# Gates' product ahead of the value projection in a two-block sequence kernel on one Trainium2 core

## The chip, the core and the metric

The program runs on one core of one Trainium2 chip. TensorE multiplies, VectorE (DVE), ScalarE (ACT) and GpSimd (POOL) do the rest, and the SyncE queue (SP) starts most of the transfers. Each engine runs its own list of instructions in order and waits for semaphores that others raise. The metric is the device time in microseconds (us) of one execution; lower is better.

## What is computed

Two transformer-like blocks over 512 tokens of width 1024, in float32. The change lies in the first block, in one wide projection and what hangs on it:

```python
h = rms_norm(x, norm_mix_g) * (1.0 + sc1) + sh1
proj = einsum("bsd,de->bse", h, w_in) + b_in
glu_in, qk_in, v, o_pre, if_pre, merge_pre = split(proj, IN_SPLITS)

a = glu_in[..., :1024] * sigmoid(glu_in[..., 1024:])
a = causal_depthwise_conv(a, conv_dw_w, conv_dw_b)       # 31 taps, 1024 channels
a = silu(layer_norm(a, conv_ln_g, conv_ln_b))            # then w_conv_pw

qk = silu(causal_depthwise_conv(qk_in, qk_conv_w, qk_conv_b))   # 4 taps
hm = mlstm_chunkwise(q, k / 16, v, i_pre, f_pre)         # 4 heads of 256
```

`mlstm_chunkwise` needs, from the 8 gate columns `if_pre`, `log_sigmoid(f_pre)` (computed as min(f, 0) - ln(1 + exp(-|f|))), its running sum b, and a running maximum m of i - b: the decays. They weigh the scores of each head.

## The kernel before

Each product with a weight is made exact enough by cutting weight and activation in a high and a low part and adding three products (high by high, low by high, high by low). Channels lie on partitions, 512 tokens side by side, so one tile of 128 output channels is 24 matmuls of 128x512 from one weight unit of 128x1024; the value projection `w_v` has tokens on partitions instead and takes four units in each of its two blocks, which fill four PSUM banks at a time.

A weight unit is loaded by SP into one of four `raw` buffers; ACT copies it to `sph` (the high part, L2103), one of three buffers. The low part `spl` is made in one of two ways: by a subtraction on DVE (L2464), or, for the units in `BY_DMA`, by a negated copy on ACT (L2106) and an adding DMA that POOL issues (L3102). The unit of the gates, `w_if`, has eight columns; its low part lies in the other half of the same `sph` buffer (L2459) and its product is 16 matmuls (L1932).

The function `plan()` writes the order by hand: it walks through the tiles, and after each third of a tile `between()` lets background work step forward: `later_ops` (operations put off by a tick), `side` (generators, one step for each tick), and `spare`, a queue of single taps of the 31-tap convolution (L2523, L2526, on DVE). `rate[1]` is the number of taps for each tick. Every engine then gets its part of this one list, in that order.

Around the change the order is this: eight pairs of convolution tiles; the value blocks 0 and 1 (units 16 to 23) with 3.2 taps a tick; the gates' product (unit 24); then head 0's tiles z = 0 to 3 (units 25 to 28), head 1's tiles from unit 29 on, and so forth. After the gates' product ACT copies one half (L2136), DVE adds the other (L2549), and ACT runs `gates` (L2142 to L2151: two biased copies, Abs, Exp, Ln, the last two each with a table load). The generator `decays()` puts `log_forget` (L2555), four steps `decay` (L2564 to L2572, one for each 128 tokens), the copies `decay_rows` (L2579, L2582, L2587) and the transposes `decay_cols` beside the tiles that follow. A head's tile goes through ACT (L2159, L2162), three taps on DVE (L2597) and ACT again (L2167). The value tiles leave their banks on DVE (L2543, `vtok`).

PSUM banks come from two rings, `main` and `misc`. Two banks are lent from `misc` to `main` during the convolution tiles and the value blocks, and go back afterwards. A tile that takes a bank waits until its last user has emptied it. `fence(name)` marks a place that other engines' first writes to reused memory wait for.

Of the kernel before, what the change touches and what calls it, by code (L numbers as in the profile page):

```python
# [24 lines left out]
for _name, _n in [("b_ada", 48), ("g_mix", 8), ("b_glu", 16), ("b_qk", 16), ("b_o", 8), ("b_mg", 16),  # L25
# [16 lines left out]

GMIX, GFFN = 0, 72

BY_DMA = (*range(6, 24),)

WHOLE = (0, 1, 2, 3,)

ATTEND = (3, 2, 0, 7)

ORDER = [(0, 0), (0, 1), (0, 2), (1, 0), (0, 3), (1, 1), (1, 2), (1, 3)]
TAPS = [[0, 0, 0, 1], [1, 1, 1, 1], [1, 1, 1, 1], [1, 1, 1, 1], [1.6, 1.6, 1.6, 1.6], [1.6, 1.6, 1.6, 1.6],
        [1.6, 1.6, 1.6, 1.6], [1.6, 1.6, 1.6, 1.6]]

LENT = 2
# [32 lines left out]
class Signals:  # L88
# [11 lines left out]
    def up(self, name, *labels, by=1):  # L100
        self.count[name] = self.count.get(name, 0) + by
        for label in labels:
            assert label not in self.now, label
            self.now[label] = (name, self.count[name])
        return self.sem(name), by

    def at(self, *label):
        if not self.known:
            return None
        name, value = self.known[label]  # L110
        return self.sem(name), value
# [18 lines left out]
def plan():  # L130
# [3 lines left out]
    def add(name, *args):  # L134
        steps.append((name, args))

    main, misc, tmp = Ring(0, 4), Ring(4, 4), Ring(0, NT)
# [8 lines left out]
    def keepc(n):  # L146
        kept[0] += n
        assert kept[0] <= 176
        return kept[0] - n

    def fence(name):
        add("fence", name)
# [6 lines left out]
    def load():  # L159
        add("load", W["loaded"])  # L160
        W["loaded"] += 1
# [3 lines left out]
    def split():  # L165
# [9 lines left out]
        if n in WHOLE:  # L175
            W["owed"] += 1
            return
        add("split", n, "dma" if n in BY_DMA else lo_engine[0])
        load()
# [32 lines left out]
    def ready(eng=None, more=0):  # L212
        was = lo_engine[0]
        lo_engine[0] = eng or was
        while W["cut"] < W["finished"] + W["ahead"] + more:
            split()
        lo_engine[0] = was

    def take(name, tile, first, size):
        units.append((name, tile, first, size))  # L220
        W["used"] += 1
        ready()
        return W["used"] - 1

    def done():
        W["finished"] += 1


    side, tail, spare, later_ops = [], [], [], []
    rate, due, tick = [0, 0], [0.0], [0]  # L230
# [18 lines left out]
    def between():  # L249
        while later_ops and later_ops[0][0] <= tick[0]:  # L250
            later_ops.pop(0)[1]()
        tick[0] += 1
        step(rate[0])
        due[0] += rate[1]
        background(int(due[0]))
        due[0] -= int(due[0])
# [3 lines left out]
    def new_tile():  # L260
        tiles[0] += 1
        return tiles[0] - 1
# [98 lines left out]
    def gemm_halves(src, acts, evac):  # L361

        b, free = main.take()
        g = new_tile()
        n = take(src, 0, 0, 1024)
        for half in range(2):
            for k0 in (0, 4):
                add("side_by_side", b, acts, n, half, k0, free, [("unit", n), ("tile", g)] * (half and k0 == 4))
                if not half:
                    if k0 == 0:  # L370
                        ready(more=1)
                    between()
        done()
        main.give(b, *evac(b, g))
        between()

    def gemm_tok(src, block, kt, acts, evac):
        banks = [main.take() for _ in range(T)]
        g = new_tile()
        for k0 in range(0, kt, 2):  # L380
            n = take(src, block, k0 * 512, 1024)
            for k in range(2):
                last = k0 + k == kt - 1
                add("tok", banks, acts, n, k, k0 + k, last, [("unit", n)] * (k == 1) + [("tile", g)] * last)
                if k == 0:
                    ready(more=1)
                    between()
            done()
            if k0 + 2 < kt:
                between()  # L390
        for t in range(T):
            main.give(banks[t][0], *evac(t, banks[t][0], g))
        between()
# [52 lines left out]
    def spread(name, src, after):  # L446
        b, bfree = misc.take()
        add("spread", name, src, b, bfree, after)
        return b
# [15 lines left out]
    def rows_of(ss, width, between=(), behind=()):  # L465
        b = spread(ss.name, ("small", root_of(ss, width, *between)), [("rs", ss.name)])
        if behind:
            warm(*behind)
        return b
# [68 lines left out]
    for i in range(8):  # L538
# [4 lines left out]
        j, free = tmp.take()  # L543
# [75 lines left out]
    fence("v")  # L619
    add("v_begin")  # L620

    for blk in range(2):
        def evac(t, b, g):
            add("v", blk, t, b, g)
            return [("v", blk, t)]
        gemm_tok("w_v", blk, 8, "n1", evac)

    def gates(b, g):
        j, free = tmp.take()
        k, free2 = tmp.take()  # L630
        add("gates_low", b, g, k, free2)
        add("gates_sum", b, j, free, k)
        later_ops.append((tick[0] + 1, lambda: add("gates", j, k)))
        forget.extend((j, k))
        return [("gate", "sum")]

    forget = []
    gemm_halves("w_if", "n1", gates)
    misc.free += [main.take() for _ in range(LENT)]
    cb, gd, mus = keepc(40), keepc(16), keepc(8)  # L640

    def decays():
        yield
        yield
        add("log_forget", *forget)
        for j in forget:
            tmp.give(j, ("lf",))
        k1, free = tmp.take()
        fence("decay")
        add("decay_begin", k1, free, mus)  # L650
        for t in range(T):
            add("decay", t, k1, mus)
            yield
        tmp.give(k1, ("decay", 3))
        add("m_out")
        for k in range(T):
            add("decay_rows", k)
            yield
        for _ in range(5):
            yield  # L660
        b, free = misc.take()
        add("decay_cols", b, free, cb, gd)
        misc.give(b, ("cb",), ("gd",))

    side.append(decays())


    fence("qk")
# [72 lines left out]
    def heads(h):  # L741
# [3 lines left out]
        for z in range(4):  # L745
            i = 2 * h + z % 2 + (8 if z >= 2 else 0)
            rate[:] = [1, TAPS[h][z]]
            used = qk_used[(h + 1) % 2] + ([("decay_tr",)] if h == 1 else [])
# [50 lines left out]
    def gates_on(h):  # L799
        for z in range(4):  # L800
            rate[:] = [1, TAPS[4 + h][z]]
            i = 2 * h + z % 2
# [262 lines left out]
    b = spread("x1", ("small", root), [("rs", "x1")])  # L1065
# [277 lines left out]
    for i in range(4):  # L1343
        b, free = misc.take()
# [50 lines left out]
    b = spread("mix", ("small", r), [("rs", "mix")])  # L1395
# [72 lines left out]
    b = rows_of(ssf, D, (320,), (512, 512))  # L1468
# [24 lines left out]
def program(nc, A, out, known):  # L1493
    steps, units = plan()
    ctx = ExitStack()
    with ctx:
# [8 lines left out]
        def place(name, off, shape, dt=F32):  # L1505
            return nc.alloc_sbuf_tensor_at(name, shape, dt, offset=base + off)
# [29 lines left out]
        TMP = [place(f"tmp{i}", o + 2048 * i, [128, S]) for i in range(NT)]; o += 2048 * NT  # L1536
# [65 lines left out]
        def vec(name, i, p=slice(0, 128)):  # L1602
            return V_[p, VEC[name] + i:VEC[name] + i + 1]
# [113 lines left out]
        def fenced(name, *engines):  # L1717
            return [at("fence", name, e) for e in engines or ("PE", "ACT", "DVE", "POOL")]
# [15 lines left out]
        def run(program_of):  # L1734
            for name, args in steps:
                if name in program_of:
                    program_of[name](*args)
# [357 lines left out]
        def _(e):  # L2095
            w = Waited(e, G)
            up, fence = follow("ACT")
# [40 lines left out]
            def gates(j, k):  # L2138
                p = slice(32, 36)
                z, y = TMP[j], TMP[k]  # L2140
                w.wait_ge(at("gate", "sum"), *fenced("v"))
                e.activation(IR[:], z[0:4, :], ACT.Identity, bias=vec("b_if", 0, slice(0, 4))).then_inc(  # L2142
                    *up("s_if", ("gate", 0)))
                e.activation(z[p, :], z[p, :], ACT.Identity, bias=vec("b_if", 0, p)).then_inc(
                    *up("s_if", ("gate", 1)))
                w.wait_ge(at("gate", 1))
                e.activation(y[p, :], z[p, :], ACT.Abs).then_inc(*up("s_if", ("gate", 2)))
                w.wait_ge(at("gate", 2))
                e.activation(y[p, :], y[p, :], ACT.Exp, scale=-1.0).then_inc(*up("s_if", ("gate", 3)))
                w.wait_ge(at("gate", 3))  # L2150
                e.activation(y[p, :], y[p, :], ACT.Ln, bias=1.0).then_inc(*up("s_if", ("gate", 4)))  # L2151
# [279 lines left out]
            def pg(i, b, g, j, free):  # L2431
# [1 line left out]
                e.activation(TMP[j][:], P_[b][:], ACT.Sigmoid, bias=vec("b_pg", i)).then_inc(  # L2433
                    *up("s_gate", ("pg_gate", i)))

            run({"begin": begin, "split": split, "csil": csil, "square": square, "rsqrt": rsqrt, "root_table": root_table, "glu": glu, "gates": gates, "gates_low": gates_low, "rope_rows": rope_rows, "decay_cols": decay_cols, "qk": qk,
                 "qk_silu": qk_silu, "score": score, "vals": vals, "head_scale": head_scale, "turn": turn,
                 "gate_mul": gate_mul, "gc": gc, "gc_gate": gc_gate, "ln_mean": ln_mean, "ln_out": ln_out, "pw": pw, "norm": norm, "gmix": gmix, "round": round_,
                 "silu_table": silu_table, "seven_full": seven_full, "seven_t_high": seven_t_high, "seven_high": seven_high, "seven_first": seven_first, "seven_third_copy": seven_third_copy,
# [866 lines left out]
```

## Time and profile before

| | us |
|---|---|
| median of 3 runs | 1557.66 |
| lowest, highest | 1556.52, 1559.5 |
| the profiled execution | 1556.89 |
| its span in the trace | 1555.1 |

Mean granted clock of TensorE: 0.992 of full. Busy shares of the span: TensorE's matmuls 98%, weight loads 83%, DVE 73%, ACT 52%, POOL 10%, DMA queues together about 46% of the 16 engines. The time of the profiled execution is the span and 1.8 us around it. In a timeline each row is a run of equal instructions: its start, its length, engine, line, what it writes and reads and how many; brackets name the idle time before it and who ended that. A matmul's end is modelled, so a row of matmuls is longer than the distance to the next one's start.

### The profile page before, as it was taken

The numbers are of one execution on the slowest core, as the hardware profiler recorded it, in microseconds if no ns is written. First come the engines' busy times: TensorE is split into PE (matmuls) and PEld (weight loads), VectorE is DVE, ScalarE is ACT, GpSimd is POOL, SyncE is SP. The second block draws the span as 40 slices with busy tenths as digits, with TensorE's granted clock in tenths as the row PEclk, the third lists the DMA queues.
The fourth block names the chain that finished last, engine by engine and source line by source line (L and its number), as shares of the span: only waits on it lengthen the run. The fifth ranks groups of instructions, "written<-read, shape, count | busy, mean of one in ns | idle before, by whom it ended". The sixth has DMA issues, their size and how long they took to land.

```text
span 1555.1 us, 21650 instructions
## 1 busy us (share of the span) xinstructions
PE 1522.9 (98%) x8256; PEld 1297.4 (83%) x8256; DVE 1140.3 (73%) x1852; ACT 805.1 (52%) x1292; POOL 151.3 (10%) x158
## 2 busy tenths in 40 slices
PE   8999899999999999999899999999999999999998
PEld 3788777877888899999688887778887999998877
DVE  8998898898788789888464447766578888854356
ACT  5543578765543656666333335446456666643223
POOL 0111000000000101111011001000202111100000
PEclk9999999999999999999999999999999999999999
DMA  9788221222566547755533323110325555573331
GB/s 371 178 188 208 69 95 61 75 95 90 209 237 209 162 123 198 196 150 156 160 111 91 119 74 118 63 48 28 115 82 184 150 150 158 156 236 116 98 135 68
DMA packets 66490, 215.17 MB, mean 138 GB/s; under 512 B 7757, under 2 KB 10061, under 8 KB 65618
## 3 DMA queue, kind: packets, MB, share of 16 engines
q1 hardware_dynamic: 52496, 179.68, 33.8%
q0 software_dynamic: 13888, 34.09, 11.4%
q8 instruction: 66, 1.08, 0.3%
q14 instruction: 38, 0.31, 0.1%
q10 hardware_dynamic: 2, 0.00, 0.0%
HBM read 175.99 MB, written 8.40 MB: 119 GB/s over the span
## 4 chain that ended last, share of the span: by engine, by line
PE 47%; DVE 3%; ACT 1%; issue 1%; DMA 1%; SPq 0%; DVEq 0%; ACTq 0%
PE bank L1875 10%; PE bank L1876 10%; PE bank L1883 9%; PE bank L1913 4%; PE bank L1915 4%; PE bank L1923 4%; PE bank L2045 1%; PE bank L2058 1%; DMA tmp<-in_pos 1%; PE bank L2051 1%; PE bank L2072 1%; PE bank L2065 1%; PE bank L1953 0%; PE bank L1954 0%; PE bank L1955 0%
## 5 line engine op out<-in xcount | busy, mean ns | idle before, releaser
L1875 PE MATMUL bank<-HH,sph 128*128 128x512 f32 x840 | 339.5, 404 | 9.4 <-DVE spl L2464 7.7
L1876 PE MATMUL bank<-HH,spl 128*128 128x512 f32 x840 | 330.0, 393 | 0.0
L2464 DVE TENSOR_TENSOR spl<-raw,sph 128x1024 fp32r<-128x1024 f32 (+2 forms) x162 | 201.5, 1246 | 161.6 <-ACT sph L2103 161.4
L2103 ACT ACTIVATE sph<-raw 128x1024 fp32r<-128x1024 f32 (+1 forms) x183 | 187.1, 1025 | 163.0 <-PE bank L1883 124.0
L1883 PE MATMUL bank<-HL,sph 128*128 128x512 f32 x840 | 222.8, 397 | 0.0
L1875 PEld LDWEIGHTS bank<-HH,sph 128*128 128x128 f32 x840 | 159.4, 190 | 47.2 <-issue 11.9
L1876 PEld LDWEIGHTS bank<-HH,spl 128*128 128x128 f32 x840 | 159.4, 190 | 34.5 <-issue 1.4
L1883 PEld LDWEIGHTS bank<-HL,sph 128*128 128x128 f32 x840 | 156.6, 188 | 34.8 <-issue 2.4
L2526 DVE SCALAR_TENSOR_TENSOR convout<-convin,vecs,convout 128x512 f32<-128x512 f32 x240 | 165.0, 745 | 0.0
L1913 PE MATMUL bank<-HH,sph 128*128 128x256 f32 x592 | 148.7, 283 | 0.1
L1915 PE MATMUL bank<-HH,spl 128*128 128x256 f32 x592 | 148.4, 283 | 0.0
L1875 PE MATMUL bank<-midh,sph 128*128 128x512 f32 x352 | 138.0, 392 | 7.2 <-DVE spl L2464 7.2
L1876 PE MATMUL bank<-midh,spl 128*128 128x512 f32 x352 | 137.7, 391 | 0.0
L1913 PEld LDWEIGHTS bank<-HH,sph 128*128 128x128 f32 x592 | 113.6, 192 | 0.7 <-ACT tmp L2282 0.5
L1915 PEld LDWEIGHTS bank<-HH,spl 128*128 128x128 f32 x592 | 113.6, 192 | 0.1
L1913 PE MATMUL bank<-th,sph 128*128 128x256 f32 x444 | 111.5, 283 | 0.2 <-ACT tmp L2277 0.2
L1915 PE MATMUL bank<-th,spl 128*128 128x256 f32 x444 | 111.3, 283 | 0.0
L2776 DVE TENSOR_TENSOR spl<-raw,sph 128x512 fp32r<-128x512 f32 x148 | 100.0, 696 | 10.7 <-ACT sph L2272 10.6
L2272 ACT ACTIVATE sph<-sums 128x512 fp32r<-128x512 f32 x111 | 65.1, 621 | 71.5 <-DVE sums L2763 71.5
L1923 PE MATMUL bank<-HL,sph 128*128 128x256 f32 x592 | 95.2, 283 | 0.0
L2272 ACT ACTIVATE sph<-raw 128x512 fp32r<-128x512 f32 x148 | 92.2, 623 | 4.2 <-PE bank L1923 1.2
L1883 PE MATMUL bank<-midl,sph 128*128 128x512 f32 x352 | 87.6, 389 | 0.0
(365 smaller groups left out, 2715.5 us busy)
## 6 DMA issues: line engine op xcount, KB each, us to landing
raw<-in_w_in SPq DMA_DIRECT2D x69, 512.0 KB, 3.3
raw<-in_w_up SPq DMA_DIRECT2D x66, 512.0 KB, 4.5
more<-in_w_ada SPq DMA_DIRECT2D x32, 512.0 KB, 5.4
raw<-in_w_down SPq DMA_DIRECT2D x32, 512.0 KB, 3.7
raw<-in_w_gate SPq DMA_DIRECT2D x22, 512.0 KB, 3.6
raw<-raw POOLq DMA_DIRECT2D x37, 256.0 KB, 4.4
midl<-tmp POOLq DMA_DIRECT2D x37, 256.0 KB, 3.3
spl<-raw POOLq DMA_DIRECT2D x18, 512.0 KB, 5.9
```

Of the source, the lines that this page charges most:

```text
L1875: e.matmul(P_[b][:], sph(n)[:, q], hi[:, k, :], start=k == 0, stop=False)
L1876: e.matmul(P_[b][:], spl(n)[:, q], hi[:, k, :], start=False, stop=False)
L1883: m = e.matmul(P_[b][:], sph(n)[:, q], low[:, k, :], start=False, stop=last and k == kb - 1)
L1913: e.matmul(to, high_of(which, s)[:, q], x, start=begins and k == 0, stop=False, skip_group_check=not begins)
L1915: e.matmul(to, low_of(which, s)[:, q], x, start=False, stop=False, skip_group_check=not begins)
L1923: m = e.matmul(to, high_of(which, s)[:, q], x, start=False, stop=k == 3, skip_group_check=not begins)
L2045: e.matmul(P_[b][:, 0:wide], QH[:, h, token(t)], KH[:, h, 0:wide], start=True, stop=True).then_inc(*up("s_score", ("mla_mm", h, t)))
L2103: e.activation(sph(n), raw(n), ACT.Copy).then_inc(*up("s_w_high", ("wh", n)))
L2272: e.activation(high_of(which, s), given, ACT.Copy).then_inc(*up("s_w_high", ("seven_high", which, s), *labels))
L2464: e.tensor_tensor(spl(n), raw(n), sph(n).bitcast(F32), ALU.subtract).then_inc(*up("s_w_low", ("wl", n)))
L2526: ins = e.scalar_tensor_tensor(CO[:, i, :], src, wt, CO[:, i, :], ALU.mult, ALU.add)
L2776: e.tensor_tensor(low_of(which, s), given, high_of(which, s).bitcast(F32), ALU.subtract).then_inc(*up("s_w_low", ("seven_low", which, s), ...
```

## The change

The gates' product goes from behind the value blocks to ahead of them, so `w_if` is now unit 16 and the value units are 17 to 24; `BY_DMA` moves with that, and the number of units cut by DMA stays 18. Of the gates' activations the Exp and Ln stand two ticks later than the first three, in a step of their own (`gates_log`). `decays()` starts beside value block 0. The taps beside the value blocks go from 3.2 a tick to 1.5 (gates' product), 1.4 (block 0) and 3.2 (block 1), and the tiles of head 0 get 1.3, 1.3, 1.3 and 2.3 a tick where they had 0, 0, 0 and 1. The two lent banks go back after value block 1.

```diff
-BY_DMA = (*range(6, 24),)
+BY_DMA = (*range(6, 16), *range(17, 25),)
...
-TAPS = [[0, 0, 0, 1], [1, 1, 1, 1], [1, 1, 1, 1], [1, 1, 1, 1], [1.6, 1.6, 1.6, 1.6], [1.6, 1.6, 1.6, 1.6],
+VALUE_TAPS = (1.4, 3.2)
+TAPS = [[1.3, 1.3, 1.3, 2.3], [1, 1, 1, 1], [1, 1, 1, 1], [1, 1, 1, 1], [1.6, 1.6, 1.6, 1.6], [1.6, 1.6, 1.6, 1.6],
...
-    for blk in range(2):
-        def evac(t, b, g):
-            add("v", blk, t, b, g)
-            return [("v", blk, t)]
-        gemm_tok("w_v", blk, 8, "n1", evac)
...
         later_ops.append((tick[0] + 1, lambda: add("gates", j, k)))
+        later_ops.append((tick[0] + 3, lambda: add("gates_log", k)))
...
+    rate[:] = [1, 1.5]
     gemm_halves("w_if", "n1", gates)
-    misc.free += [main.take() for _ in range(LENT)]
...
     def decays():
-        yield
-        yield
+        k1, free = tmp.take()
+        fence("decay")
+        add("decay_begin", k1, free, mus)
+        for _ in range(4):
+            yield
         add("log_forget", *forget)
         for j in forget:
             tmp.give(j, ("lf",))
-        k1, free = tmp.take()
-        fence("decay")
-        add("decay_begin", k1, free, mus)
...
     side.append(decays())
+
+    for blk in range(2):
+        def evac(t, b, g):
+            add("v", blk, t, b, g)
+            return [("v", blk, t)]
+        rate[:] = [1, VALUE_TAPS[blk]]
+        gemm_tok("w_v", blk, 8, "n1", evac)
+
+    misc.free += [main.take() for _ in range(LENT)]
...
+            def gates_log(k):
+                p, y = slice(32, 36), TMP[k]
                 w.wait_ge(at("gate", 2))
                 e.activation(y[p, :], y[p, :], ACT.Exp, scale=-1.0).then_inc(*up("s_if", ("gate", 3)))
```

What this makes of the order is seen best on DVE, beside value block 1. Names there: `vtok<-bank` empties a value block, `convout<-convin` is a tap, `spl<-raw,sph` the low part of a weight unit, `sph_60<-raw_54` that of the gates' unit. Before, from block 0's emptying to block 1's:

```order
L2543 TENSOR_TENSOR vtok<-bank,vbias 128x2x256 x4
L2526 SCALAR_TENSOR_TENSOR convout<-convin,vecs,convout 128x512 x16
L2459 TENSOR_TENSOR sph_60<-raw_54,sph_60 128x8x64
L2537 TENSOR_TENSOR tmp_90<-tmp_90,convout 128x512 x2
L2523 TENSOR_SCALAR convout<-convin,vecs 128x512 x2
L2526 SCALAR_TENSOR_TENSOR convout<-convin,vecs,convout 128x512 x3
L2464 TENSOR_TENSOR spl_61<-raw_55,sph_58 128x1024
L2526 SCALAR_TENSOR_TENSOR convout<-convin,vecs,convout 128x512 x3
L2543 TENSOR_TENSOR vtok<-bank,vbias 128x2x256 x4
```

Now the same stretch begins with block 0's emptying, the fourth decay step (four instructions) and a tap, and its last 12 groups, from the second of four copies `decay_rows` (`rowc<-`) on, are:

```order
L2587 COPY rowc<-row_138 4x128
L2590 TENSOR_SCALAR rowc<-rowc,row_137 4x128 x2
L2534 SCALAR_TENSOR_TENSOR convout<-convin,vecs,convout 128x512 x4
L2587 COPY rowc<-row_138 4x128
L2590 TENSOR_SCALAR rowc<-rowc,row_137 4x128
L2534 SCALAR_TENSOR_TENSOR convout<-convin,vecs,convout 128x512 x3
L2587 COPY rowc<-row_138 4x128
L2595 TENSOR_TENSOR row_135<-mrow,row_137 4x512
L2534 SCALAR_TENSOR_TENSOR convout<-convin,vecs,convout 128x512 x3
L2472 TENSOR_TENSOR spl_61<-raw_55,sph_58 128x1024
L2534 SCALAR_TENSOR_TENSOR convout<-convin,vecs,convout 128x512 x6
L2472 TENSOR_TENSOR spl_62<-raw_56,sph_59 128x1024
```

Behind these stand four taps and then the emptying of block 1. In all 24 taps, one decay step, all of `decay_rows` and two low parts stand between the two emptyings, where 22 taps, two first taps (L2523), two sums, one low part of a unit and that of the gates stood before.

On DVE at the first head tiles, before, behind the low part of unit 27 (`spl_63`):

```order
L2597 SCALAR_TENSOR_TENSOR tmp_91<-xpad,vecs,tmp_91 128x512 x3
L2555 SCALAR_TENSOR_TENSOR row_136<-tmp_86,tmp_88 4x512
L2564 SCALAR_TENSOR_TENSOR row_137<-tmp_89,row_136 4x128
L2567 TENSOR_TENSOR row_138<-row_135,row_137 4x128
L2569 SCALAR_TENSOR_TENSOR mrow<-row_138,kept 4x128
L2572 TENSOR_TENSOR kept<-mrow,row_137 4x1
L2464 TENSOR_TENSOR spl_61<-raw_54,sph_58 128x1024
```

Now, from the emptying of value block 1 to the same low part of unit 28:

```order
L2551 TENSOR_TENSOR vtok<-bank,vbias 128x2x256 x4
L2545 TENSOR_TENSOR tmp_90<-tmp_90,convout 128x512 x2
L2531 TENSOR_SCALAR convout<-convin,vecs 128x512 x2
L2472 TENSOR_TENSOR spl_63<-raw_57,sph_60 128x1024
L2534 SCALAR_TENSOR_TENSOR convout<-convin,vecs,convout 128x512
L2599 COPY kept<-bank 128x40
L2534 SCALAR_TENSOR_TENSOR convout<-convin,vecs,convout 128x512
L2605 SCALAR_TENSOR_TENSOR tmp_89<-xpad,vecs,tmp_89 128x512 x3
L2534 SCALAR_TENSOR_TENSOR convout<-convin,vecs,convout 128x512 x2
L2472 TENSOR_TENSOR spl_61<-raw_54,sph_58 128x1024
```

The decay steps are gone from this place, and taps stand in it. On PE the first tile of head 0 (unit 25) waited for the second of block 1's four `vtok` instructions before; the rings now hand it a bank that the first of the four empties.

## Rows read from the trace of the kernel before

**Rows 1.** The page: busy time, share of the span, instructions.

```profile
PE 1522.9 (98%) x8256; PEld 1297.4 (83%) x8256; DVE 1140.3 (73%) x1852; ACT 805.1 (52%) x1292; POOL 151.3 (10%) x158
```

**Rows 2.** TensorE's waits, whole span: total, times, longest.

```profile
PE bank L1875 <- DVE spl L2464: 14.9, 3, 7.2
```

**Rows 3.** TensorE's timeline at head 0's tiles: start, length.

```profile
158.04 0.39 PE L1875 MATMUL bank<-HH,sph 128*128 128x512 f32 x1
...
172.54 1.98 PE L1883 MATMUL bank<-HL,sph 128*128 128x512 f32 x8
179.27 0.77 PE L1875 MATMUL bank<-HH,sph 128*128 128x512 f32 x1 [4.75 <-DVE spl L2464]
...
187.38 0.39 PE L1875 MATMUL bank<-HH,sph 128*128 128x512 f32 x1
```

**Rows 4.** Windows after two stalls: busy of PE, PEld, DVE, ACT, POOL; clock; DMA.

```profile
179.27:187.38 8.11, 8.11 (x24) 6.51 (x25) 7.60 (x19) 2.97 (x4) 0.55 (x1) 0.66 0.21 66
1190.46:1196.46 6.00, 6.00 (x19) 4.79 (x20) 5.72 (x8) 2.48 (x5) 2.41 (x2) 0.72 0.33 102
```

**Rows 5.** TensorE's timeline at a shorter stall, later in the program.

```profile
1190.46 0.47 PE L1875 MATMUL bank<-HH,sph 128*128 128x512 f32 x1 [2.99 <-DVE spl L2464]
```

**Rows 6.** DVE's timeline at the head tiles and decays.

```profile
173.10 2.33 DVE L2597 SCALAR_TENSOR_TENSOR tmp<-xpad,vecs,tmp 128x512 f32<-128x512 f32 x3 [4.54 <-ACT tmp L2162]
...
184.05 0.41 DVE L2564 TENSOR_TENSOR_SCAN row<-tmp,row 4x128 f32<-4x128 f32 x1
...
185.39 1.21 DVE L2464 TENSOR_TENSOR spl<-raw,sph 128x1024 fp32r<-128x1024 f32 x1
186.53 0.21 DVE L2579 COPY rowc<-row 4x128 f32<-4x128 f32 x1
...
188.35 2.31 DVE L2597 SCALAR_TENSOR_TENSOR tmp<-xpad,vecs,tmp 128x512 f32<-128x512 f32 x3
190.57 0.21 DVE L2579 COPY rowc<-row 4x128 f32<-4x128 f32 x1
...
191.02 1.21 DVE L2464 TENSOR_TENSOR spl<-raw,sph 128x1024 fp32r<-128x1024 f32 x1
192.16 0.21 DVE L2579 COPY rowc<-row 4x128 f32<-4x128 f32 x1
...
192.90 1.40 DVE L2526 SCALAR_TENSOR_TENSOR convout<-convin,vecs,convout 128x512 f32<-128x512 f32 x2
```

**Rows 7.** DVE's timeline beside value block 1.

```profile
132.85 2.48 DVE L2543 TENSOR_TENSOR vtok<-bank,vbias 128x512 f32<-128x512 f32 x4 [4.63 <-PE bank L1955]
135.25 10.68 DVE L2526 SCALAR_TENSOR_TENSOR convout<-convin,vecs,convout 128x512 f32<-128x512 f32 x16
145.85 0.69 DVE L2459 TENSOR_TENSOR sph<-raw,sph 128x512 fp32r<-128x512 f32 x1
...
154.61 2.48 DVE L2543 TENSOR_TENSOR vtok<-bank,vbias 128x512 f32<-128x512 f32 x4 [0.66 <-PE bank L1955]
```

**Rows 8.** ACT's timeline: the gates' Exp and Ln.

```profile
167.64 1.28 ACT L2149 ACT_TABLE_LOAD   x1
...
170.88 0.63 ACT L2151 ACTIVATE tmp<-tmp 4x512 f32<-4x512 f32 x1
```

**Rows 9.** TensorE's timeline in value block 0: the wait for unit 18.

```profile
121.63 0.50 PE L1953 MATMUL bank<-sph,HH 128*128 128x512 f32 x1 [0.61 <-DMA spl<-raw]
```

**Rows 10.** POOL's timeline: the issue of unit 18's adding DMA.

```profile
113.67 0.86 POOL L3102 DMA_DIRECT2D spl<-raw  x1 [0.32 <-issue]
```

**Rows 11.** Line L3102 from 90 to 150, its ten adding DMAs: time to landing.

```profile
DMA to landing us min/median/max: 4.6/6.1/7.9
```

**Rows 12.** TensorE's waits from 200 to 450: the two longest.

```profile
PE bank L2039 <- DVE tmp L2537: 0.8, 1, 0.8
PE bank L2028 <- DVE sc L2612: 0.8, 1, 0.8
```

**Rows 13.** Window around a TensorE wait of 1.42, columns as in rows 4.

```profile
1030.00:1036.00 6.00, 4.58 (x25) 3.38 (x24) 4.93 (x13) 3.05 (x8) 1.10 (x1) 1.00 0.15 48
```

More of the change, by code:

```diff
@@ L2434, in pg @@
                     *up("s_gate", ("pg_gate", i)))
-            run({"begin": begin, "split": split, "csil": csil, "square": square, "rsqrt": rsqrt, "root_table": root_table, "glu": glu, "gates": gates, "gates_low": gates_low, "rope_rows": rope_rows, "decay_cols": decay_cols, "qk": qk,
+            run({"begin": begin, "split": split, "csil": csil, "square": square, "rsqrt": rsqrt, "root_table": root_table, "glu": glu, "gates": gates, "gates_log": gates_log, "gates_low": gates_low, "rope_rows": rope_rows, "decay_cols": decay_cols, "qk": qk,
                  "qk_silu": qk_silu, "score": score, "vals": vals, "head_scale": head_scale, "turn": turn,
```

## The prediction

> **What bounds the kernel now.** The page comes first: TensorE is busy for 98% of the span [rows 1], so a change can give back only what TensorE idles, and what it loses at a lower clock behind an idle stretch. Next come TensorE's waits by cause: the longest group is three waits for low parts of weights cut on DVE, 14.9 us in all [rows 2]. The three lie at different places; the timeline of the head tiles holds the one this change aims at. There the last matmuls of unit 27 begin at 172.54, and unit 28 begins only at 179.27, after 4.75 idle [rows 3]. The pace: from 158.04 to 172.54 are 64 matmuls in 14.5 us, 0.2266 each, so a unit of 24 is 5.44 and the eight from 172.54 end at 174.35. The stall is 4.92 from issue to issue. The unit behind it takes 187.38 - 179.27 = 8.11 instead of 5.44, at a granted clock of 0.66 on average [rows 4]: 2.67 more, the first part of it at 1.2 GHz. Together 7.59 us.
>
> Why it is there: DVE sat idle 4.54 us until 173.10 for ACT's first qk copy [rows 6], which stood behind the gates' activations with two table loads, 167.64 to 171.51 [rows 8]; behind it DVE ran the logarithm's sum, a decay step, and then unit 28's low part.
>
> **What is removed.** The gates and most decay steps leave the head tiles, so that chain is broken. What comes late instead is counted below. Unit 28's low part now has before it on DVE (from the order) the emptying of block 1 (2.40, 132.85 to 135.25 [rows 7]), some sums and taps, one low part and three qk taps. I follow that further down; it comes out ahead of TensorE. Gain: 7.59.
>
> **What is added: the emptying of value block 1.** This is the main term. Call T0 the time at which TensorE ends block 0. DVE begins to empty it some 0.2 later (132.85 against 132.65, which is 158.04 less 16 and 96 matmuls at 0.2266) and is done 2.40 later. Up to the emptying of block 1 the order gives DVE:
> - 24 taps at 0.6625 (16 from 135.25 to 145.85 [rows 7]): 15.90
> - one decay step, 184.05 to 185.39 [rows 6]: 1.34
> - the copies `decay_rows`: 186.53 to 188.35 is 1.82, 190.57 to 191.02 is 0.45, 192.16 to 192.90 is 0.74 [rows 6]: 3.01
> - two low parts at 1.14 (185.39 to 186.53 [rows 6]): 2.28
>
> The sum is 22.53. Block 1's emptying so begins at T0 + 25.13, its first bank is free after a quarter of 2.48, at T0 + 25.75, and TensorE starts 0.15 after its releaser, as at 179.27. TensorE ends block 1 after 96 matmuls, at T0 + 21.76, and unit 25 needs just that bank (the order: the first of the four, where it was the second before). So TensorE stands still for 25.90 - 21.76 = 4.14 us from issue to issue. Before, DVE was ready 0.66 early at this place [rows 7]. Idle time that DVE has in block 0 does not help, because the chain begins with T0. Both ends of this term lie close: with every dependent step 0.03 shorter it is 3.6; I take 4.14.
>
> **The clock behind it.** A stall of 2.99 [rows 5] was followed by six microseconds at 0.72 [rows 4], a loss of 6 x 0.28 = 1.7; the one of 4.75 cost 2.67. Idle 4.0 (4.14 less the tail of the last matmul) lies between: I take 2.2, bounds 1.7 and 2.7.
>
> **Unit 18.** In block 0 TensorE now waits 0.61 for unit 18's adding DMA [rows 9], issued by POOL at 113.67 [rows 10] and landed 7.9 later, the slowest of the ten [rows 11]. It shares the DMA engines with the next weight load and the bias of the values. POOL's issue hangs on ACT's copies behind the last convolution gate and on a fence there, and neither moves. But the gates' 16 matmuls take 3.63 where unit 16 took 5.44, so TensorE is at unit 18 1.81 earlier. If it lands as late as before, the wait is 0.61 + 1.81 = 2.42; if in the median 6.1, 0.62; in 4.6, none. One adding DMA before it is gone and the load behind unit 17 can start earlier, so I take a landing 1.1 earlier than before, a wait of 1.3. Term: +0.7, bounds -0.6 and +1.8. A wait of 1.42 cost no clock (1.00 [rows 13]); at 2.4 it may, another 1.7 by rows 4, which goes in the upper bound.
>
> A sentence apart: the Trainium skill, DMA: Bandwidth & Descriptors, section Anatomy of one DMA, gives a transfer that GpSimd issues 2.0 us and its bytes over 436 GB/s. As an estimate by that page 512 KB take 3.2 us, unit 18 lands at 116.9, and this term would be -0.6 instead of +0.7. Its section Issuing engines are not separate DMA queues says that transfers of all queues interleave on the same 16 engines; the 7.9 of rows 11 against 4.6 speaks for the second, and no landing in rows 11 is as short as the first.
>
> **The gates' activations and the decays in block 0** cost nothing on the path. ACT runs the first three after DVE's sum of the gates at about 115.5, then one unit's copies, then Exp and Ln in 3.87 (167.64 to 171.51 [rows 8]) from about 121.4 to 125.3. DVE has eight taps (5.3) meanwhile and idles some 4.5. Then `log_forget` and three decay steps with four taps (0.6 + 3 x 1.34 + 4 x 0.66 = 7.3) end at about 132.7, ahead of T0 = 113.9 + 21.8 + 1.3 = 137.0. That cover is 4 us; without it each microsecond moves block 1 one to one. POOL's first write of the decays waits for its fence ahead of unit 20's DMA, by about 118.8; ACT has that unit's copies done at 121.4. The store of m stands ahead of unit 24's DMA and waits for the fourth decay step, T0 + 4, while unit 24's copies end after T0 + 7.5. Unit 16's low part is now cut on DVE at about 101, nine microseconds before it is used.
>
> **The taps in head 0.** With 1.3 taps a tick a tile holds four: DVE needs 4 x 0.66 + 1.14 + 2.22 (the three qk taps, 188.35 to 190.57 [rows 6]) = 6.0 for each 5.44 of TensorE, and for z = 3 seven taps, 8.0. Over four tiles it falls back 26.0 - 21.8 = 4.2. I count from unit 25's start U: low part of unit 28 at U + 14.0, needed at U + 18.5 (with 2.2 for the clock); unit 30: 25.4 against 29.4; unit 31: 33.3 against 34.9; unit 32: 39.3 against 40.3. The margin sinks to about 1 us and no more is asked of it, since from head 1 on the numbers of taps are as before. Cost 0, and a rival.
>
> **Later.** Two taps a tick fewer beside the values are made up one tile later, and the layer norm starts two ticks, 3.6 us, later in TensorE's order. Its mean was waited for 0.8 [rows 12]; DVE's work up to there is the same, so that wait goes: -0.8, bounds 0 and -0.8. The 0.8 beside the scores [rows 12] may go or stay: 0, bounds -0.8 and 0.
>
> **Sum.** -7.59 + 4.14 + 2.2 + 0.7 - 0.8 = -1.35 us. The profiled execution took 1556.89, so it would take 1555.5; the median of the runs lies 0.8 above it, and against that the forecast is 1556.3. All low bounds: -7.6 + 3.6 + 1.7 - 0.6 - 0.8 - 0.8 = -4.5; all high: -7.6 + 4.14 + 2.7 + 1.8 + 1.7 = +2.8. Own range 1553.2 to 1560.4.
>
> **Rivals.**
> - *The stall goes and none comes.* If DVE's row of small decay steps runs much faster between independent taps than alone, and it reaches block 1's bank by T0 + 21.8, the sum is -7.59 + 0.7 - 0.8 = -7.7: 1550.0. Against it: 15.9 of taps and 2.3 of low parts alone leave 1.0 for steps that took 4.35.
> - *Unit 18 lands in time*, with the 4.6 of rows 11: its term is -0.6 for +0.7, the sum -2.65, 1555.0. For it: less traffic before. Against it: the slowest landing was this one. The figure of the Trainium skill's page on DMA, named above, would have it come out so.
> - *Slower: head 0's taps make a second stall.* The margin at units 31 and 32 is 1 us. If DVE comes there more than that late (a longer stall does not help it, a qk copy on ACT that comes late hurts it), TensorE waits again. Price: some 3.0 idle as in rows 5 and 1.7 of clock, 4.7: -1.35 + 4.7 = +3.4, 1561.0. It decides from 1 us of delay on DVE. For it: DVE is over its share in all four tiles. Against it: the count above, by rows, stays positive at each unit.
>
> **How the numbers follow.** Forecast 0.58; no stall 0.13; unit 18 in time 0.15; second stall 0.14. A measurement of this kernel can tell about 0.2%, 3.1 us, from no change. Faster by more than that: all of the first rival, 0.13, four tenths of the second, 0.06, and 0.09 of the forecast's low end: 0.28. Slower: six tenths of the third, 0.08, and 0.02: 0.10. Between: 0.62. The range reaches down to the first rival and up to the middle of the third: 1550.0 to 1560.8.
>
> **What would show it.** In the profile after: TensorE's timeline with one wait of about 4 in front of the first tile of head 0, released by DVE's `vtok`, and a clock near 0.7 behind it; no wait of 4.75 for unit 28; a wait of 0 to 2.4 in block 0 at the second value unit; DVE idle some 4 us in block 0 for the Ln. Wrong would make it: `vtok` of block 1 beginning less than 21.6 us after block 0's end, or any wait for a low part at units 28 to 33.

## The result, and the profile after

Eight runs of each kernel: before 1557.34 us in the median (1556.21 to 1560.54), after 1563.70 (1560.42 to 1566.09). The ratio is 1.0036, with a 95% interval of 1.0024 to 1.0047: slower, by 6.4 us in the medians. The forecast was 1556.3 with a range up to 1560.8; the measured time lies above it. The profiled execution of after took 1561.86 (span 1560.0), 4.97 more than that of before, and the steps are accounted against that difference.

First the page of after, against [rows 1]. The busy times are as good as equal (TensorE 1524.3 for 1522.9), so no work was added; TensorE stands still for longer.

```profile
PE 1524.3 (98%) x8256; PEld 1297.3 (83%) x8256; DVE 1140.7 (73%) x1852; ACT 803.9 (52%) x1291; POOL 150.5 (10%) x158
```

TensorE's waits over the span (total, times, longest), against [rows 2]. DVE's low parts went from 14.9 to 11.9: the 4.75 at unit 28 is gone, and three small waits (1.03, 0.26, 0.21) came. Of the two causes beside them the first is new, and the second had 0.6 before:

```profile
PE bank L1880 <- DVE spl L2472: 11.9, 5, 7.4
PE bank L1880 <- DVE vtok L2551: 4.0, 1, 4.0
...
PE bank L1958 <- DMA spl<-raw: 2.4, 1, 2.4
```

In TensorE's timeline they are the second value unit of block 0 (unit 18, [rows 9] had 0.61 there) and the first tile of head 0 (unit 25, no wait in [rows 3]). Unit 28 now begins without one, unit 29 likewise:

```profile
121.21 0.50 PE L1958 MATMUL bank<-sph,HH 128*128 128x512 f32 x1 [2.41 <-DMA spl<-raw]
165.17 0.50 PE L1880 MATMUL bank<-HH,sph 128*128 128x512 f32 x1 [3.96 <-DVE vtok L2551]
184.41 0.39 PE L1880 MATMUL bank<-HH,sph 128*128 128x512 f32 x1
189.86 0.39 PE L1880 MATMUL bank<-HH,sph 128*128 128x512 f32 x1
```

Behind each of the two waits the granted clock fell from 2.4 to 1.2 GHz for a while: the matmuls behind unit 18's wait start 0.43 us apart, and from 125 us on 0.23 again. Windows of ten us, columns as in [rows 4]; the clock stands third from the end. 0.83 of ten us is a loss of 1.7 us, twice:

```profile
120.00:130.00 10.00, 8.79 (x31) 7.07 (x32) 5.24 (x13) 6.16 (x7) 0.86 (x1) 0.83 0.84 202
160.00:170.00 10.00, 6.04 (x20) 4.55 (x19) 9.90 (x16) 2.34 (x2) 0.00 (x0) 0.83 0.15 54
```

DVE beside the value projection, against [rows 7]. It waits for ACT's Ln (the gates' logarithm), then for the end of block 0, and is late at the end of block 1 (164.45):

```profile
124.95 0.68 DVE L2563 SCALAR_TENSOR_TENSOR row<-tmp,tmp 4x512 f32<-4x512 f32 x1 [4.51 <-ACT tmp L2159]
139.50 2.49 DVE L2551 TENSOR_TENSOR vtok<-bank,vbias 128x512 f32<-128x512 f32 x4 [7.09 <-PE bank L1960]
164.45 2.46 DVE L2551 TENSOR_TENSOR vtok<-bank,vbias 128x512 f32<-128x512 f32 x4
```

Unit 18's adding DMA, against [rows 10, 11]: issued 0.4 earlier than before (113.26), and as slow as before.

```profile
DMA to landing us min/median/max: 7.9/7.9/7.9
```

**Where the 4.97 us lie.** Start times of the same matmuls in both traces, before in the first fence, after in the second: the first tile of the convolutions, the 14 small matmuls that turn the decays, and the first matmul of the third tile of a later projection.

```profile
44.26 0.79 PE L1875 MATMUL bank<-HH,sph 128*128 128x512 f32 x1
...
194.73 0.78 PE L2012 MATMUL bank<-consts,rowc 4*128 4x4 f32 x10
...
438.90 0.39 PE L1875 MATMUL bank<-ah,sph 128*128 128x512 f32 x1
```

```profile
43.87 0.79 PE L1880 MATMUL bank<-HH,sph 128*128 128x512 f32 x1
...
170.64 0.78 PE L2017 MATMUL bank<-consts,rowc 4*128 4x4 f32 x10
...
443.02 0.47 PE L1880 MATMUL bank<-ah,sph 128*128 128x512 f32 x1 [0.21 <-DVE spl L2472]
```

The difference is -0.4 at 44, +7.1 at unit 25 (158.04 in [rows 3], 165.17 now), +2.5 at unit 29 (187.38 and 189.86), of which 1.2 are the small matmuls that now stand ahead of it, and +4.1 at 439. Each step by the prediction's terms:

| term | forecast | in the traces |
|---|---|---|
| stall of unit 28 and the clock behind it | -7.6 | -7.6 |
| emptying of block 1 | +4.1 | +4.1 |
| clock behind it | +2.2 | +1.7 |
| unit 18: the wait | +0.7 | +1.8 |
| unit 18: clock behind it | 0 | +1.7 |
| heads 1 to 3 up to 439 | -0.8 | +2.8 |
| ahead of the first convolution tile | 0 | -0.4 |
| from 439 to the end | 0 | +0.9 |
| sum | -1.4 | +5.0 |

### The profile page after: what moved, and what is told of

Read it like the earlier page. It is cut to its first block, busy times and chain, and to the rows that moved or that the text cites. A ratio compares the mean times of both kernels' runs of the same rounds, so it can differ in the third digit from the quotient of the medians.

```text
span 1560.0 us, 21648 instructions
## 1 busy us (share of the span) xinstructions
PE 1524.3 (98%) x8256; PEld 1297.3 (83%) x8256; DVE 1140.7 (73%) x1852; ACT 803.9 (52%) x1291; POOL 150.5 (10%) x158
## 4 chain that ended last, share of the span: by engine, by line
PE 47%; DVE 2%; ACT 1%; DMA 1%; issue 1%; SPq 0%; DVEq 0%; ACTq 0%
PE bank L1880 10%; PE bank L1881 10%; PE bank L1888 10%; PE bank L1918 4%; PE bank L1920 4%; PE bank L1928 4%; PE bank L2050 1%; PE bank L2063 1%; DMA tmp<-in_pos 1%; PE bank L2056 1%; PE bank L2077 1%; PE bank L2070 1%; PE bank L1958 0%; PE bank L1960 0%; PE bank L1959 0%
## 5 line engine op out<-in xcount | busy, mean ns | idle before, releaser
L1880 PE MATMUL bank<-HH,sph 128*128 128x512 f32 x840 | 340.2, 405 | 10.7 <-DVE spl L2472 4.3
L2108 ACT ACTIVATE sph<-raw 128x1024 fp32r<-128x1024 f32 (+1 forms) x183 | 187.2, 1025 | 160.1 <-PE bank L1888 123.3
L2784 DVE TENSOR_TENSOR spl<-raw,sph 128x512 fp32r<-128x512 f32 x148 | 100.1, 697 | 10.7 <-ACT sph L2280 10.6
```

The source lines that it names most:

```text
L1880: e.matmul(P_[b][:], sph(n)[:, q], hi[:, k, :], start=k == 0, stop=False)
L2108: e.activation(sph(n), raw(n), ACT.Copy).then_inc(*up("s_w_high", ("wh", n)))
L2784: e.tensor_tensor(low_of(which, s), given, high_of(which, s).bitcast(F32), ALU.subtract).then_inc(*up("s_w_low", ("seven_low", which, s), ...
```

## The experiments

The experiments were timed in three groups, each beside runs of before of its own: 1557.67 (27 runs) for e1 to e4, 1558.61 (17) for e5 to e8, 1557.84 (15) for e9 to e11. Differences to after are between medians of different groups, so a microsecond of them says nothing. The ratio behind each time is to before, with its 95% interval in brackets.

### e1: taps out of block 1

```
-VALUE_TAPS = (1.4, 3.2)
+VALUE_TAPS = (2.4, 2.2)
```

> The kernel after with the rates of the taps beside the value blocks at 2.4 and 2.2 a tick for 1.4 and 3.2: seven taps go from block 1 to block 0, where DVE idled 4.51 and 7.09 us. Theory A (the chain of DVE in block 1 sets the wait for its first bank): the wait of 3.96 ahead of head 0 goes to 0, and so does the half clock behind it (some 1.8 us); against the kernel after -5.8 us, 1557.9. Rival B (the wait only moves: DVE has as much to do up to unit 28, and the tiles of head 0 come 5.8 us earlier on TensorE than on DVE): the bank's wait goes, but waits for low parts of 2 to 5 us come at units 28 to 33, gain 0 to 3 us, 1561 to 1564. The wait of 2.41 for unit 18 stays under both.

Measured: 1558.01 (1556.18 to 1559.89), ratio to before 1.0000 [0.9991, 1.0009]; 5.7 below after, for the 5.8 of theory A. TensorE's timeline:

```profile
122.86 0.50 PE L1958 MATMUL bank<-sph,HH 128*128 128x512 f32 x1 [2.44 <-DMA spl<-raw]
162.04 0.50 PE L1880 MATMUL bank<-HH,sph 128*128 128x512 f32 x1 [0.79 <-DVE vtok L2551]
```

The bank's wait fell by 3.2, not to 0 as theory A had it, and no wait came at units 28 to 33: rival B falls. Unit 18's wait is there as before, but this time the clock stayed full behind it:

```profile
120.00:130.00 10.00, 7.56 (x33) 5.92 (x32) 8.00 (x16) 7.20 (x8) 0.86 (x1) 1.00 0.96 218
```

### e2: unit 18's low part on DVE

```
-BY_DMA = (*range(6, 16), *range(17, 25),)
+BY_DMA = (*range(6, 16), 17, *range(19, 25),)
```

> The kernel after with one number taken out of the list of adding DMAs: unit 18's low part is cut on DVE (1.14 us more there, in idle time). Theory A: the wait of 2.41 us in block 0 and the half clock behind it (1.7) go, -4.1 us against the kernel after, 1559.6; the bank of block 1 is waited for as before (3.96), since its chain begins with the end of block 0. Rival C (the time that block 0 gains is lost to later waits, since ACT's Ln and DVE's decay steps keep their time): the decay chain has 4 us of cover against the earlier end of block 0, so C gives 0 to -2: 1562 to 1564.

Measured: 1558.79 (1557.31 to 1561.27), 1.0004 [0.9995, 1.0013]; 4.9 below after, for 4.1 expected. No wait in block 0, and the bank's as after:

```profile
161.04 0.50 PE L1880 MATMUL bank<-HH,sph 128*128 128x512 f32 x1 [3.97 <-DVE vtok L2551]
```

Unit 25 begins 4.13 earlier than in after (165.17). That is the price of this one wait with its clock. Rival C falls.

### e3 and e11: both edits

> Both edits, rates of 2.4 and 2.2 and unit 18's low part on DVE. Theory A: the two add up, -5.8 - 4.1 = -9.9 us against the kernel after, 1553.8, and 3.5 below the kernel before (1557.3). If the small later waits (3.5 us after, 2.0 before) are the rest of the loss, they stay. Rival B or C: the sum is less than its parts, 1558 or more.

> e3_both once more, beside e9_side_late and e10_bias_side on one chip, so that differences of 1 us can be read: 1553 to 1554.5 by its first median (1553.0) and that of e8_best (1555.3), which had the same waits.

Measured: 1553.02 (1552.03 to 1555.48), 0.9968 [0.9955, 0.9980], and again 1553.66 (1552.55 to 1556.82, 11 runs), 0.9976 [0.9967, 0.9985]. The two edits add up to -10.7 and -10.0 against after (9.9 expected), and this kernel is faster than both. So the change as it stands loses some 10 us at two places of the value projection, and once these are mended it gains over 4 us. What is left in TensorE's timeline up to 300:

```profile
158.06 0.50 PE L1880 MATMUL bank<-HH,sph 128*128 128x512 f32 x1 [0.78 <-DVE vtok L2551]
239.68 0.50 PE L1880 MATMUL bank<-HH,sph 128*128 128x512 f32 x1 [0.28 <-ACT xpad L2167]
271.57 0.50 PE L1880 MATMUL bank<-HH,sph 128*128 128x512 f32 x1 [0.58 <-ACT tmp L2206]
299.06 0.47 PE L1880 MATMUL bank<-HH,sph 128*128 128x512 f32 x1 [1.02 <-DVE spl L2472]
```

### e4: the bias load out of the adding DMA's way

`v_begin` on SP is the load of the values' bias, 512 KB, broadcast to 128 partitions. It is split off and comes in the decays' second step:

```
-        for _ in range(4):
+        for n in range(4):
+            if n == 1:
+                add("bias_load")
             yield
```

> The kernel after with SP's load of the value bias (a broadcast to 128 partitions) moved from ahead of the value projection to behind the issue of unit 18's weights. Theory D (unit 18's adding DMA is slow because the bias load and the next weight load share the DMA engines with it): it lands 1 to 3 us earlier than its 7.9 us, TensorE's wait of 2.41 becomes 0 to 1.4 and the clock behind it stays full; -2.7 to -4.1 us, 1559.6 to 1561. Rival E (the landing is set by when POOL issues it and by the weight loads alone): wait and time as in the kernel after, 1563.7.

Measured: 1559.36 (1556.18 to 1561.23), 1.0006 [0.9995, 1.0016]; 4.3 below after. Nothing of unit 18 was touched, only the load beside it (issued at 122.64 now). Its adding DMA, issued at 113.5, now took:

```profile
DMA to landing us min/median/max: 4.4/4.4/4.4
```

for 7.9, and TensorE doesn't wait for it. Theory D holds and rival E falls: the bias load, issued at 112.7 in after, cost the adding DMA 3.5 us. It is not the only thing that makes such a DMA slow: in before the one issued at 96.4 took 7.8 with no bias load near it, and what slowed that one was not tried.

### e5 and e6: each part alone

e5 has the gates ahead, with the taps' rates of before:

```
-VALUE_TAPS = (1.4, 3.2)
-TAPS = [[1.3, 1.3, 1.3, 2.3], ...
+VALUE_TAPS = (3.2, 3.2)
+TAPS = [[0, 0, 0, 1], ...
...
-    rate[:] = [1, 1.5]
+    rate[:] = [1, 3.2]
```

> One part of the change alone: gates' product, activations and decays ahead of the value projection, the adding DMAs as after, but the rates of the taps as before (3.2 a tick at the gates and beside both value blocks, none in the first three tiles of head 0). Theory A (two places in the value blocks carry the loss; the taps in head 0 cost nothing): block 1 has as many taps on DVE as after, so the waits of 2.41 for unit 18 and of about 4 for the bank stay, each with half clock behind; block 0 takes 17 taps more, 11.3 us, against 11.6 of idle time there, so it comes out level: time as the kernel after, 1563 (1561 to 1565). Rival F (the taps moved to head 0 cause the small waits later, 3.5 us after against 2.0 before): those waits go back to 2.0 or below and the time falls by 1.5 or more, 1561 or less.

Measured: 1563.54 (1562.59 to 1564.24), 1.0031 [1.0020, 1.0043], as after. The wait for unit 18 was 2.53. The waits behind it up to 320:

```profile
140.68 0.50 PE L1958 MATMUL bank<-sph,HH 128*128 128x512 f32 x1 [0.54 <-DVE vtok L2551]
167.22 0.79 PE L1880 MATMUL bank<-HH,sph 128*128 128x512 f32 x1 [5.84 <-DVE vtok L2551]
250.84 0.50 PE L1880 MATMUL bank<-HH,sph 128*128 128x512 f32 x1 [0.26 <-ACT xpad L2167]
282.75 0.50 PE L1880 MATMUL bank<-HH,sph 128*128 128x512 f32 x1 [0.61 <-ACT tmp L2206]
310.24 0.47 PE L1880 MATMUL bank<-HH,sph 128*128 128x512 f32 x1 [1.02 <-DVE spl L2472]
```

The 17 taps more in block 0 didn't come out level: its emptying was late, and the wait behind block 1 grew to 5.84, where 4 was expected. The waits at 250.84, 282.75 and 310.24 stand with the old rates too, so rival F falls for them: they come with the gates' place, not with the taps. It doesn't fall altogether. The two waits of 0.26 and 0.21 that after has at 403 and 443 are not in e5, and the one for the mean is 0.84 as before, not 1.00: up to 0.6 us of waits may hang on the rates (the one at 403 is missing in e2 and e3 too).

e6 has the gates behind the values, as before, with the taps' rates of after (the rate set in the loop over the value blocks, `TAPS[0]` as after):

```
     for blk in range(2):
+        rate[:] = [1, (1.4, 3.2)[blk]]
```

> The other part alone: the kernel before, its gates behind the value projection, with the taps' rates of the kernel after (1.4 beside block 0, 3.2 beside block 1, 1.3 and 2.3 in head 0). Theory A: head 0 now holds taps and decays together. Four taps (2.65 us) fall into the 4.54 of idle time ahead of the first qk taps, the next four lie ahead of unit 28's low part, so its stall grows from 4.75 by some 2.6 to 7.4, and behind it DVE has about 7.3 us a tile (6.0 and a decay step of 1.34) for TensorE's 5.44, so a further wait of 1 to 4 comes by unit 31: 1562 to 1567. Rival G (the taps slip into idle time, as between dependent steps): as before, 1557.5.

Measured: 1568.85 (1566.32 to 1570.30), 1.0064 [1.0052, 1.0077], slower than the upper end expected (1567). At units 28, 29 and 30:

```profile
181.22 0.77 PE L1876 MATMUL bank<-HH,sph 128*128 128x512 f32 x1 [6.16 <-DVE spl L2465]
191.24 0.47 PE L1876 MATMUL bank<-HH,sph 128*128 128x512 f32 x1 [1.44 <-DVE spl L2465]
199.55 0.47 PE L1876 MATMUL bank<-HH,sph 128*128 128x512 f32 x1 [2.59 <-DVE spl L2465]
```

The stall of unit 28 grew by 1.4 (2.6 expected), and two more followed, 4.0 together, where one of 1 to 4 was expected. Rival G falls. The taps fit into head 0 only once the decays have left it.

### e7: the gates' activations in one part

```
-        later_ops.append((tick[0] + 3, lambda: add("gates_log", k)))
+        later_ops.append((tick[0] + 1, lambda: add("gates_log", k)))
```

> The kernel after with the gates' activations in one part: Exp and Ln follow the gates' first two activations at once, ahead of the copies of unit 20's weights. The chain of DVE in block 0 ends ahead of block 0's end in either order, so theory A expects no difference, 1563.7. If the start of the decays did matter (rival), Ln ends some 2.4 us earlier and up to 2.4 us would be gained, 1561.3; if unit 20's adding DMA, issued 3 us later, did, TensorE would wait for it in block 0.

Measured: 1563.03 (1559.67 to 1564.04), 1.0022 [1.0012, 1.0032]; 0.7 below after with ranges that overlap. The two places are as in after (below). Neither rival's sign is there: nothing is gained that can be measured, and TensorE doesn't wait for unit 20.

```profile
122.91 0.80 PE L1958 MATMUL bank<-sph,HH 128*128 128x512 f32 x1 [2.72 <-DMA spl<-raw]
166.77 0.57 PE L1880 MATMUL bank<-HH,sph 128*128 128x512 f32 x1 [3.97 <-DVE vtok L2551]
```

### e8: one tap more out of block 1

As e3, with `VALUE_TAPS = (2.6, 2.0)`.

> As e3_both (unit 18's low part on DVE, rates 2.4 and 2.2), with rates of 2.6 and 2.0: one tap (0.66 us) more goes out of the chain of block 1, where e3_both still waited 0.78, into block 0, where DVE still idled 0.74 and 0.73 us. Theory A: the wait for the bank becomes 0.1 to 0.2, TensorE does not wait in block 0: 0.6 below e3_both, 1552.4. Rival: block 0's emptying is now late itself, and its end moves the chain of block 1 with it: 1553 or above.

Measured: 1555.28 (1551.86 to 1556.11), 0.9974 [0.9962, 0.9986]; not told apart from e3. The wait did not shrink, and TensorE has none in block 0. TensorE first, DVE below:

```profile
157.70 0.50 PE L1880 MATMUL bank<-HH,sph 128*128 128x512 f32 x1 [0.78 <-DVE vtok L2551]
```

```profile
156.96 2.48 DVE L2551 TENSOR_TENSOR vtok<-bank,vbias 128x512 f32<-128x512 f32 x4 [0.68 <-PE bank L1960]
```

DVE is now early and waits 0.68 for TensorE's last matmuls of block 1, and TensorE still waits 0.78 for the first bank. Neither theory had this: with DVE early, 0.78 is still what is left in the new order. Unit 25 wants a bank of the block that just ended, and the gates' 16 matmuls (3.6 us), which lay between the two before, no longer cover its emptying.

### e9 and e10: the attention's place

e9 is e3 with empty steps behind the decays on the side queue, so that head 0's attention takes its first step as late as in before:

```
         misc.give(b, ("cb",), ("gd",))
+        for _ in range(14):
+            yield
```

> As e3_both, with 14 empty steps at the end of the side queue's decays, so that the attention of head 0 takes its first step as late as in the kernel before (without them the side queue is free 14 ticks earlier, and the attention's steps stand elsewhere between the tiles of the heads 1 to 3 on every engine). Theory H (this earlier place makes the small waits of 0.28, 0.58 and 1.02 us at units 31 to 43, which all kernels with the gates ahead have and neither kernel with the gates behind has): they go, the 0.8 beside the scores that the kernel before had comes back, 1 us below e3_both's own repetition. Rival I (they come from the rotation of the scratch tiles or from one tap more or less): they stay, no difference.

Measured: 1552.93 (1551.63 to 1554.03), 0.9968 [0.9955, 0.9980]; 0.7 below e11, inside the ranges. In TensorE's timeline up to 350 the three waits of e3 are gone, and the one from before is back at 0.60:

```profile
208.61 0.67 PE L2035 MATMUL bank<-vtok,sc 128*128 128x257 f32 x2 [0.60 <-DVE sc L2622]
308.42 1.10 PE L2027 MATMUL bank<-qk 128*128 128x512 f32 x2 [0.35 <-ACT qk L2177]
```

ACT in e3 shows how such a wait comes about: it stands 3.75 for the norms of a head, and the high copy of the next weights (L2108, 296.61) is queued behind. In before and in e9 the copy for the same unit (295.72 and 288.60) stands ahead of the norms' table load.

```profile
288.75 1.28 ACT L2128 ACT_TABLE_LOAD   x1
293.78 0.20 ACT L2128 ACTIVATE small<-small 128x4 f32<-128x4 f32 x1 [3.75 <-DVE small L2492]
294.62 2.08 ACT L2195 ACTIVATE htok<-htok,small 128x256 f32<-128x256 f32 x4 [0.64 <-DVE small L2650]
296.61 1.04 ACT L2108 ACTIVATE sph<-raw 128x1024 fp32r<-128x1024 f32 x1
```

Theory H holds for the waits. The median can't show what it gains, but the traces can. From unit 25 to the third tile of the later projection TensorE needs 276.4 us in e3 (158.06 to 434.43), 276.1 in e1, 276.0 in e11 and 275.8 in e8, but 274.9 in e9 (158.52 to 433.42) and 275.0 in e10, which has the empty steps too: some 1.1 us, of which the listed waits account for 1.0 (3.6 in e11, 2.6 in e9).

```profile
434.43 0.47 PE L1880 MATMUL bank<-ah,sph 128*128 128x512 f32 x1 [0.21 <-DVE spl L2472]
...
433.42 0.47 PE L1882 MATMUL bank<-ah,sph 128*128 128x512 f32 x1 [0.22 <-DVE spl L2474]
```

e10 is e4 with the rates 2.4 and 2.2 and the empty steps:

> The rates of 2.4 and 2.2 and the empty steps, but unit 18's low part left to its adding DMA, and the bias load moved behind it as in e4_bias. Theory A and D: the adding DMA lands some 4.4 after its issue, no wait in block 0, 0.78 at the bank as in e3_both; time as e9_side_late within 1 us. If the bias, now loaded later, were late for block 0's emptying, DVE would wait for its DMA there and the time would be 1 to 4 us longer.

Measured: 1552.42 (1551.36 to 1553.83), 0.9965 [0.9952, 0.9977], the lowest median, level with e9. The adding DMA landed after 4.4 again, the bias was in time. Two independent cures of unit 18's wait, less DMA beside it or no DMA for it, give the same time.

## Why the prediction was wrong, point by point

- **The old stall** (-7.6): right. Unit 28 has no wait. Its low part began at 178.88 on DVE and was done 1.1 later, 14.9 behind unit 25's start for 14.0 worked out.
- **The emptying of block 1** (+4.1) and **the clock behind it** (+2.2): right in mechanism and size, 3.96 idle and 1.7. The chain of DVE was counted at 25.13 from the end of block 0; block 0's `vtok` begins at 139.50 and block 1's at 164.45, 24.95 apart, for 24.93 by that count. e1 gave back 3.2 of the wait, and the clock behind it, by moving seven taps. That this term nearly ate the gain was foreseen.
- **Unit 18** (+0.7): the step that failed first. The prediction took a landing 1.1 earlier, because one adding DMA before it was gone and a load could start earlier. It landed in 7.9, as in [rows 11], and the wait was 2.41, the bound that the text had given as "if it lands as late as before". The clock behind it, 1.7, had been left to the upper bound. Together 3.5 for 0.7: 2.8 of the miss. e4 shows what the slow landing hangs on: not on the adding DMAs before it but on the bias load beside it, and that the change leaves beside it. The Trainium skill, DMA: Bandwidth & Descriptors, section Issuing engines are not separate DMA queues, says that DMAs interleave on the same 16 engines whoever issues them; by that rule the bias load can be expected to slow the adding one, and the traces agree (7.9 beside it, 4.4 without). The prediction named the bias load as a sharer and then reasoned with another.
- **The wait of the layer norm's mean and the scores** (-0.8): wrong in sign. The mean's wait stayed (1.0 for 0.8), and from unit 29 to 439 the traces differ by 2.8, of which 1.5 are listed waits (3.5 for 2.0); the other 1.3 lie in issue distances that no listed wait covers. That makes 3.6 of the miss, and only part of it has a shown cause. The mean stands two ticks later in TensorE's order, but so does the sum it waits for in DVE's (begun at 380.36, for 373.80 before), and DVE has no idle time in the 15 us ahead of it in either trace. So the 0.8 had no ground. The prediction also overlooked that the side queue comes free earlier, by which head 0's attention stands elsewhere between the tiles on all engines: e9 and e10 give back 1.1 by that alone. Without stall or low clock the stretch from unit 25 takes 273.3 in before (280.86 less 7.59) and 276.2 in after (277.85 less 1.7). In e5, with the old rates of the taps, it takes 274.7 (276.90 from 167.22 to 444.12, less 2.2 of clock), so in its one trace the rates have a part too, and it may overlap with the other. Some 1.7 us are left in e9 and e10, 1.0 of them in no listed wait; what makes them stays open.
- **The gates' activations and decays in block 0** (0): right. DVE idled 4.51 for Ln (4.5 worked out) and 7.09 for the end of block 0, for a cover of 4 counted; the block ended later by unit 18's wait. e7 changed nothing.
- **The taps in head 0** (0): right for head 0. No wait at units 28 to 33. Unit 31's low part began on DVE at 198.28 and was done at 199.5, and TensorE began the unit at 203.49: 4.0 ahead, where 1.6 was counted, since the count had left out the attention's first matmuls, which stand between the units there. e6 is the rival's stall, and shows that it comes only with the decays still there.
- **From profile to median**: the forecast added the 0.8 of before. The medians differ by 6.4, the profiled executions by 5.0, so the profiled one of after was among its faster. The run of after at 1560.42 had a mean clock of 0.994, that at 1566.09 one of 0.991.

The step that failed is thus two terms of the sum: unit 18's landing, taken as 1.1 shorter and measured as long as before (with the low clock behind the wait, which the sum left out), and heads 1 to 3, taken at -0.8 and measured at +2.8. These two (2.8 and 3.6) and the 0.9 after 439, less 0.5 of clock and 0.4 at the start, take the sum from -1.4 to +5.0. The 0.9 and the 0.4 have no cause that was looked for. The upper end of the range had unit 18's 3.5 in it; what it did not have was any bound above zero for the heads 1 to 3, nor a median that lies further above the profiled execution than before.

## What to carry to other kernels

When work is taken out from between two stages, ask what it covered: here the gates' matmuls had hidden the emptying of the last value banks, and the shorter stage now in front brought TensorE 1.8 us earlier to a DMA that was already late. The slow transfer stayed slow (7.9 us) as long as its neighbour on the DMA engines stayed: name the neighbour before counting on an earlier landing. And a generator that leaves a shared side queue earlier moves all that queues behind it, here over a hundred microseconds later.

## What the runs showed of the hardware

A wait of TensorE of middle length costs clock in some executions and not in others. In the profiled executions the 2.41 (after) and 2.72 (e7) in block 0 were followed by 1.7 us of loss, the 2.44 (e1) and 2.53 (e5) by none; the waits of 3.96 and more beside head 0 all were, the 0.78 none. The stall near 1190 is nearly the same in all 13 traces, 2.97 to 3.07. Behind it nothing was lost in four (e5, e8, e9, e11), 1.7 us in five (before, after, e2, e4, e7) and some 3 in four (e1, e3, e6, e10). Even the wait of 1.42 of [rows 13], which cost nothing there and in 11 other traces, was followed by a loss of 1.7 in e4. First e9, then e1, each from its stall on, then e4 around its 1.42:

```profile
1186.10 0.47 PE L1882 MATMUL bank<-HH,sph 128*128 128x512 f32 x1 [3.07 <-DVE spl L2474]
...
1186.00:1196.00 10.00, 8.59 (x48) 7.44 (x48) 9.10 (x13) 5.39 (x11) 3.08 (x3) 1.00 0.31 80
...
1191.00:1201.00 10.00, 9.52 (x34) 7.82 (x35) 9.01 (x13) 4.32 (x8) 2.41 (x2) 0.68 0.30 80
...
1030.00:1040.00 10.00, 8.59 (x39) 6.33 (x37) 7.15 (x17) 3.55 (x10) 1.26 (x1) 0.83 0.15 54
```

So the price of one such wait is read from several executions, not from one. The times of one kernel go with its mean clock: in e3 it was 0.993 in the run of 1555.48 and 0.998 in that of 1552.03. What decides whether the clock falls was not tried.
